# Seven-product pairs of an MLP: the sixth product's addition before the block sums of the next pair

## The reference

```python
def first_block(...):
    ...
    h = h + jnp.square(jax.nn.relu(_rms_norm(h, norm_ff_g[l]) @ ff_w1[l])) @ ff_w2[l]
    ...
def swiglu(x, w_gate, w_up, w_down):
    return (jax.nn.silu(x @ w_gate) * (x @ w_up)) @ w_down
...
def second_block(...):
    ...
        x = layer_norm(ALPHA * x + swiglu(x, ffn_w_gate[layer], ffn_w_up[layer], ffn_w_down[layer]),
                       ln_ffn_g[layer], ln_ffn_b[layer])
```

## Time and profile before

| | us |
|---|---|
| median of 3 runs | 1979.66 |
| lowest, highest | 1979.62, 1983.26 |
| the profiled execution | 1982.12 |
| its span | 1980.3 |
| TensorE busy in the span | 1933.5 |
| VectorE busy in the span | 1138.6 |
| ScalarE busy in the span | 811.9 |
| GpSimd busy in the span | 346.9 |

### The profile page before, as it was taken

How to read it: one execution, slowest core, us unless ns; L and a number is a source line. 1 busy time by engine, 2 the same in 40 slices (tenths; PEclk the granted TensorE clock), 3 DMA queues, 4 the chain that set the end, 5 groups by cost and what they waited for, 6 DMA issues and landing times.

```text
span 1980.3 us, 29944 instructions
## 1 busy us (share of the span) xinstructions
PE 1933.5 (98%) x12504; PEld 1283.7 (65%) x12504; DVE 1138.6 (57%) x1547; ACT 811.9 (41%) x1313; POOL 346.9 (18%) x355
## 2 busy tenths in 40 slices
PE   8999999999998999999999999999999999999997
PEld 5655655757675654886567666648766586666576
DVE  6666776655477742245757766523555667656324
ACT  6343311534354531133535444412564545444223
POOL 1011111410133320024011511101500124111101
PEclk9999999999999999999999999999999999999999
DMA  7221200233212322322230323323111023232221
GB/s 249 86 70 59 86 22 22 86 128 107 107 65 85 128 90 102 107 107 86 78 115 22 128 86 128 107 88 147 43 65 50 37 86 107 86 128 86 107 107 43
DMA packets 28240, 179.83 MB, mean 91 GB/s; under 512 B 2960, under 2 KB 7184, under 8 KB 7184
## 3 DMA queue, kind: packets, MB, share of 16 engines
q1 hardware_dynamic: 27312, 170.93, 24.2%
q10 hardware_dynamic: 512, 4.94, 0.7%
q0 software_dynamic: 288, 2.10, 0.3%
HBM read 175.86 MB, written 2.10 MB: 90 GB/s over the span
## 4 chain that ended last, share of the span: by engine, by line
PE 66%; DVE 2%; ACT 1%; issue 0%; ACTq 0%; DVEq 0%
PE psum_a L422 16%; PE psum_a L423 16%; PE psum_a L424 16%; PE psum_b L422 4%; PE psum_b L424 4%; PE psum_b L423 4%; PE psum_b L559 2%; PE psum_a L1125 0%; PE psum_b L1171 0%; PE psum_a L1190 0%; PE psum_b L570 0%; PE psum_a L1238 0%; PE psum_b L850 0%; PE psum_a L1245 0%; PE psum_den L1171 0%
## 5 line engine op out<-in xcount | busy, mean ns | idle before, releaser
L2010 DVE SCALAR_TENSOR_TENSOR W_PARTS<-W,W_PARTS 128x2048 f16<-128x2048 f32 x111 | 254.7, 2296 | 299.7 <-ACT W_PARTS L1346 299.6
L1346 ACT ACTIVATE W_PARTS<-W 128x2048 f16<-128x2048 f32 x111 | 211.0, 1904 | 275.0 <-PE psum_a L424 272.7
L422 PE MATMUL psum_a<-U,W_PARTS 128*128 128x512 f16 (+1 forms) x808 | 303.0, 375 | 1.4 <-DVE U L2130 1.4
L423 PE MATMUL psum_a<-U,W_PARTS 128*128 128x512 f16 (+1 forms) x808 | 302.7, 375 | 0.0
L424 PE MATMUL psum_a<-U,W_PARTS 128*128 128x512 f16 (+1 forms) x808 | 302.4, 374 | 0.0
L422 PE MATMUL psum_a<-ARENA,W_PARTS 128*128 128x256 f16 (+1 forms) x860 | 268.5, 312 | 2.9 <-DVE ARENA L2659 2.3
L424 PE MATMUL psum_a<-ARENA,W_PARTS 128*128 128x256 f16 (+1 forms) x860 | 268.5, 312 | 0.0
L423 PE MATMUL psum_a<-ARENA,W_PARTS 128*128 128x256 f16 (+1 forms) x860 | 268.5, 312 | 0.0
L2966 POOL TENSOR_TENSOR ARENA<-ARENA 128x512 f16<-128x512 f32 x76 | 117.5, 1553 | 440.5 <-ACT ARENA L1480 440.4
L424 PEld LDWEIGHTS psum_a<-U,W_PARTS 128*128 128x128 f16 x808 | 79.4, 98 | 91.2 <-issue 1.4
L422 PEld LDWEIGHTS psum_a<-U,W_PARTS 128*128 128x128 f16 x808 | 79.6, 98 | 88.5 <-issue 5.5
(11 more groups left out here) (376 smaller groups left out, 4059.5 us busy)
## 6 DMA issues: line engine op xcount, KB each, us to landing
W<-weights SPq DMA_DIRECT2D x159, 1024.0 KB, 4.8
CON<-const ACTq DMA_DIRECT2D x1, 3071.5 KB, 11.2
X<-x_in SPq DMA_DIRECT2D x4, 256.0 KB, 4.0
X<-x_in SPq DMA_DIRECT2D x1, 1024.0 KB, 8.0
U<-dft POOLq DMA_DIRECT2D x1, 1024.0 KB, 5.4
ARENA<-dft POOLq DMA_DIRECT2D x1, 1024.0 KB, 5.5
U<-mem_in ACTq DMA_DIRECT2D x1, 1024.0 KB, 4.8
y_out<-U SPq DMA_DIRECT2D x2, 512.0 KB, 2.9
```

What stands on the lines that cost most here:

```text
L422: nc.tensor.matmul(out, left(0), right(0), start=first, stop=False, skip_group_check=goes_on)
L423: nc.tensor.matmul(out, left(0), right(1), start=False, stop=False, skip_group_check=goes_on)
L1346: nc.scalar.activation(HOMES[home_of[g]][:, 0, :], W[g % 2][:, :], ACT.Copy, scale=W_SCALE).then_inc(sem("panel_high"), 1)
L2010: nc.vector.scalar_tensor_tensor(out=home[:, 1, :], in0=W[g % 2][:, :], scalar=W_SCALE, in1=home[:, 0, :], op0=ALU.mult, op1=ALU.subtract) ...
```

## The change

No instruction is added or removed; two lists are reordered, in `mlp` of ScalarE and of VectorE. On VectorE the block sums of the next pair move from the end of a pair's list to behind add_part 2 of the pair before, and raw_low behind them; in a GLU finish 0 comes before add_part 2. In FF the squaring of the first pair's plain tiles (`hidden(2)`) moves from the first pair's end into the second's list, behind raw_low. On ScalarE, in a GLU, the high part of the finished tile (`hidden_high(..., (0,))`) moves ahead of the high part of the sums; in FF the high parts of the first pair's plain tiles move behind it.

```diff
@@ -1507,9 +1507,14 @@
                 before = None
                 for plain, seven in M.pairs:
                     raw_high(M, seven)
+                    if before and M.gated:
+                        hidden_high(M, before[1], (0,))
                     sums_high(M, seven)
                     if before:
-                        hidden_high(M, before[1], (0,))
+                        if not M.gated:
+                            if before[1] == 3:
+                                hidden_high(M, 2)
+                            hidden_high(M, before[1], (0,))
                         if not M.gated:
                             tile_21(M, before)
                         plain_tile(M, plain, 0)
@@ -1529,7 +1534,7 @@
                         v_high(M, (V7, V4))
                         for j in range(1 if M.gated else 2):
                             hidden_high(M, j)
-                    if not M.gated:
+                    if before and not M.gated:
                         hidden_high(M, plain[1])
                     before = seven
                 split(panel_of[(M.name,) + before] + 2)
@@ -2315,9 +2320,15 @@
                 for n, (plain, seven) in enumerate(M.pairs):
                     if before:
                         add_part(M, before, 1)
+                        if M.gated:
+                            finish(M, before, 0)
+                        add_part(M, before, 2)
+                        block_sums(M, seven)
                         raw_low(M, seven)
-                        finish(M, before, 0)
-                        add_part(M, before, 2)
+                        if not M.gated:
+                            if n == 1:
+                                hidden(M.pairs[0][0][1])
+                            finish(M, before, 0)
                         sums_low(M, seven)
                         finish(M, before, 1)
                         rest_low(M, seven)
@@ -2335,11 +2346,9 @@
                         v_made(M, src, V7)
                         v_made(M, src, V4)
                         v_low(M, (V7, V4))
-                    if not M.gated:
+                    if before and not M.gated:
                         hidden(plain[1])
                     add_part(M, seven, 0)
-                    if n + 1 < len(M.pairs):
-                        block_sums(M, M.pairs[n + 1][1])
                     before = seven
                 add_part(M, before, 1)
                 finish(M, before, 0)
```

## The result

The changed kernel takes 1964.13 us (median of 4 runs, 1963.38 to 1966.35), the kernel before 1981.38 beside it (4 runs, 1979.62 to 1983.26): a ratio of 0.9913 with a 95% interval of 0.9901 to 0.9925, 17.3 us less. The profiled execution's span went from 1980.3 to 1962.5 us, 17.8 less.

The account below looks back on a forecast made before the run. TensorE's three first-pair waits for VectorE's `add_part`, with the low clock, were taken as the winnable excess, 20.49 us. Gains of 8.3 (FF) + 10.56 (GLUs) = 18.9 us from the median 1979.66 gave 1960.8 us, range 1958.5 to 1967.5.

Parts of the forecast that it names:

- the excess of 20.49 us: First pairs of FF, GLU0, GLU1 exceed the undisturbed 19.53 us by 9.93 + 5.28 + 5.28: all a new order can win.
- the part that I gave to the clock: First pairs: low TensorE clock costs 1.2 us plus about 0.5 in FF; in GLUs, clock and restart fill 5.28 beyond 3.4.
- Step 1: FF's first pair: q7 read ahead of block sums; the 8.14 us wait at q4 and low clock go, at most −9.93.
- Step 2: FF's first pair: q1 late 1.0 us, q6 late again 1.0; taken as 1.6 in all, so FF wins 8.3.
- Step 3: First pairs of GLU0 and GLU1: wait goes, q1 has 0.8 us to spare; gain 5.28 each, 10.56 together.
- Step 4: All later pairs: chain starts after q7, spare 1.8 us in GLU and 2.7 in FF at q1; cost 0.
- Step 5: Plain tile's squaring is later only in FF's first pair, counted elsewhere; behind the last pair the old order stays; cost 0.
- The rule against it: VectorE and GpSimd block each other for whole instructions: block sum 2.19 us instead of 1.52, FF 2.0 more, forecast 1962.8.
- A: First pairs: wait moves to q1, each late by 2.0 us; 1966.8, or 1971.6 with the low clock; chance 0.18.
- B: Later pairs become VectorE's: 1.5 us late in 8 GLU pairs, 0.6 in 5 FF pairs; 1988 us; chance 0.05.
- C: Change does nothing, q4 having a second reason to wait, V4; 1979.7 us; chance 0.05 with anything else within 0.2%.

Follow-up runs that it names:

- the run with the GLUs alone: Changed kernel with FF put back in its old order, the two GLUs keeping the new one; median 1969.63 us, ratio 0.9943.
- the busy waits: Kernel before, TensorE kept busy in its three waits by 34 (FF) and 15 (each GLU) matmuls into an unread bank; 1976.41 us, ratio 0.9972.
- the run with four additions: Changed kernel with four more 128x512 additions ahead of each pair's block sums from the second pair on; 1990.19 us, ratio 1.0046.
- the run with ScalarE's other order: Changed kernel, ScalarE's second FF list with next panel's split and read of q1 before the waiting high part; one execution, 1962.90 us.
- two more additions: Changed kernel with two more 128x512 additions ahead of each pair's block sums from the second pair on; 1967.37 us, ratio 0.9931.

## Why the prediction was right, point by point

- **What bounds it, and the excess of 20.49 us.** Right: 17.92 of it went, each MLP's part by itself (the run with the GLUs alone), and the part that I gave to the clock is there (the busy waits: 5.1 us).
- **Step 1**, the read of q7: starts 1.51 us after q7 where I had 1.66 (FF's third pair in the changed kernel has 1.51 too, 631.22 − 629.71; in the pair of the earlier trace rows the read stood right behind a finish, so its 1.66 holds some of VectorE's own queue); no wait at q4, no low clock. Right.
- **Step 2**, what is late next in FF: right in its places, q1 and q6, wrong in its split and too small. I had 1.6 us; it is 2.57. Up to q1 I counted too much (0.11 late instead of 0.6 to 1.0: the first block sum took 0.90, not 1.30, and the rows overlap more than I took off). Behind q1 too little: I gave the low part of the sums and the second finish their undisturbed 1.74 and 0.68, though I had written that GpSimd gets its fifth and sixth tile later, just there. Holding GpSimd back brings the 1.9 us back. That is the term that was mis-sized. That the sum came as near as it did is in part luck: up to 0.9 us too much at q1 stand against 1.5 too little behind it (1.0 forecast, 2.46 measured).
- **Step 3**, the GLUs: 19.53 both, 5.28 gained in each. The four block sums beside the rescaling took 1.31, 0.85, 0.77 and 0.69, and q1 had 1.1 us to spare where I had 0.8.
- **Step 4**, the later pairs at no cost: right, 19.53, with 2.3 us to spare in a GLU pair by the trace (2.2 by the run with four additions) where I had 1.8. Not seen: FF's second pair would have grown by 1.28 if only the first had been cured.
- **Step 5**, the squaring and the last pair: the squaring's new place is worth 1.0 us, and behind FF's last pair nothing moved (from its last q7 to GLU0's first 382.1 us in both kernels).
- **The rule against it.** By the Trainium skill ("SBUF — State Buffer", section "Who interferes with whom") I had priced a disturbed block sum at 2.19 us. The sums took 1.53, as the row of before had it. My price was wrong in adding a whole tile's 1.50: that contained waiting of the tile's own (a tile alone takes 1.16 us in these traces, 1.60 in a row beside the sums). The rule's form, that the one which issues first holds the shared port pair for its whole instruction while the other stands, is borne out where one instruction meets one tile: 0.97 more for the sums' low part, 0.96 for the finish, 0.96 for the low part of A22/S3, and 0.96 for the panel in the run with ScalarE's other order, the same whether the instruction is 0.68 or 2.29 us long. In the changed kernel the panel's low part came up when the tile had 0.62 us left, and took 0.47 more. That is a block of time and not a shared rate.
- **The rivals.** A (the wait moves to q1) did not come: 0.11 in FF, none in the GLUs. Its premise did come in FF, at q5 and q6 instead: GpSimd disturbs VectorE in the new place too. With two more additions q1 waited as well, with the low clock in FF. B (each pair becomes VectorE's) did not come either, and the run with four additions shows its price, 0.7 us a GLU pair and 1.4 an FF pair. C is out: the read of q7 moved, and the time with it.
- **The level.** I forecast 1960.8 from a median of 1979.66. The same kernel's median over further runs lies at 1981.3 to 1982.0, and that explains 1.7 of the 3.3 us by which the forecast was low; FF's 1.0 explains another part; the rest lies within the scatter of the runs. The gain itself was forecast at 18.9 and is 17.3 by the medians, 17.8 by the spans.

## What to carry to other kernels

Where a loop's steady state is bound by one engine, look at its first iteration: compare each interval with the steady one, and the excess is both the bound of the gain and the place. Put the instruction that frees a bank for the bound engine ahead of everything that has slack, and then redo the sum with the moved work's neighbours: what GpSimd gets later disturbs whatever stands there now. Before trusting the new order, add work until it breaks: here 1.4 us a pair cost nothing from the third pair on, and 2.9 us made every pair longer. Run the old order with the same work beside it, which was not done here.

## What the runs showed of the hardware

A wait need not be as long as those of the kernel before (3.4 and 8.0 us) to bring TensorE's clock down: waits of 1.40 and 1.99 us, 6.4 us apart, went ahead of the fall in FF with two additions, while the changed kernel's wait of 1.99 alone left the clock at 1.00. And equal waits differ. With four additions TensorE waits 2.34 us at q1 in the first pair of GLU0 and 2.35 in that of GLU1; in the one the clock falls and the pair takes 1.56 us more, in the other it stays:

```profile
1097.50:1121.10 23.60, 21.26 (x134) 13.59 (x133) 17.94 (x22) 9.75 (x13) 22.31 (x21) 0.93 0.25 90
1668.43:1690.47 22.04, 19.69 (x133) 12.84 (x132) 18.32 (x22) 9.38 (x13) 22.04 (x20) 1.00 0.28 96
```

Why the one and not the other stays open; no run here tells.

VectorE's additions that take one input from psum_b were never lengthened by GpSimd: 0.41 to 0.43 us in all 81 executions of the line, before and after, among them the read of q7 at 589.58, while a GpSimd tile runs. The lengthened instructions shown above have both their inputs in SBUF.
